# RWKV-7 chunks on TensorE: inversion level 5 and the join over four quarters, decay sum and exponentials moved, 128x128 block products as 64x64 pairs

## The chip, the cores and the metric

The kernel runs on one core of one Trainium2 chip. TensorE (PE) multiplies, VectorE (DVE), ScalarE (ACT) and GpSimd (POOL) do the elementwise work, SyncE (SP) issues most transfers. The metric is the time of one execution in microseconds of the device; lower is better.

## The reference

One layer step of a hybrid decoder: a SwiGLU half step, RWKV-7 time mixing beside an S5 branch, a gated merge, a second SwiGLU half step. 1024 prompt tokens and 8 sample tokens, all in fp32. The change concerns the RWKV branch. Per head of 64 (8 heads):

```python
def step(S, inp):
    r_t, w_t, k_t, v_t, kk_t, b_t = inp
    sa = jnp.einsum('bhvk,bhk->bhv', S, -kk_t)
    S = (S * w_t[:, :, None, :] + sa[..., None] * b_t[:, :, None, :]
         + v_t[..., None] * k_t[:, :, None, :])
    o = jnp.einsum('bhvk,bhk->bhv', S, r_t)
    return S, o
...
mu = jnp.mean(o, axis=-1, keepdims=True)
var = jnp.mean(jnp.square(o - mu), axis=-1, keepdims=True)
o = ((o - mu) * lax.rsqrt(var + LNX_EPS)).reshape(B, L, W) * p['lnx_w'] + p['lnx_b']
bonus = jnp.sum(r_h * k_h * p['r_k'], axis=-1, keepdims=True) * v_h
```

## The kernel before

The prompt is cut into 8 chunks of 128 tokens. Inside a chunk the recurrence is turned into products: masked score matrices of decayed keys (`scores`), the inverse of a unit triangular 128x128 matrix per head, and products with the state. The inverse is built from 2x2 blocks upward. `first` gives blocks of 2; `level_x` and `level_t` do levels 1 to 5, each doubling the block: `level_x` multiplies the score matrix by the inverse so far, DVE copies the masked result into `g.X` (`level`, L2635), `level_t` multiplies again, for the inverse and its transpose, and ACT copies both to `g.T2` (L2373). At level 5 the two 64x64 diagonal blocks are complete; the transposes go to `g.TTF`. `join` (L2919) makes the off-diagonal 64x64 block with two products in a row, each with an ACT copy behind it (`x60`, `x61`, then `t60`, `t61`). Heads are handled as 2 groups n of 4 pairs p; group n owns PSUM banks `tb(n)` and `tb(n)+1` (6, 7 and 4, 5).

The array is used in 64x64 quarters here: a product that reads partitions 0 to 63 or 64 to 127 (`lo`, `hi`) uses that half of the rows, and one that writes PSUM partitions `lo` or `hi` that half of the columns. In `level_x` products go lo to hi and hi to lo. In `level_t` of levels 1 to 4 the first pair crosses and the second stays, so all four quarters are used; in level 5 three products of a pair all cross, two of them hi to lo. The first join product goes lo to hi only, the second hi to lo only. The bonus (`blkrk`), the centring (`T_CEN`) and the sample state sums (`T_BLK`) multiply by 128x128 matrices that are zero outside their two diagonal 64x64 blocks.

The order is written out by hand in a `turn` of each engine, for i from -1 to 8. In turn i the state and outputs of chunk s = i, the inversion of chunk q = i+1 and the preparation of chunk p = i+2 (decays, keys, bonus, gate) are interleaved. Within a turn each engine runs its list in order; semaphores with named events tie the lists. Waits that matter:

- `lora(p)` (L2797) is the first group of a turn on PE. It waits for `bv` of p-1, the bonus values that DVE writes at the end of the turn before (`bonus`, L2615), since both use the same bank.
- On DVE the end of a turn is `level(q,5)`, `decayed_pair(p)`, `inverse_decayed(p)` (event `kr`, which the next `scores` wait for), `bonus(p)`.
- `scores(q,p)` on PE wait for the join's last copy of the chunk before (`t61`), and p = 2, 3 for DVE's mask of p-2. `first(q)` waits for the fourth mask (`score3`).
- DVE's `decay_sum(p)` (L2554) is a running sum over the tokens; it stands between `advance(s)` and `level(q,2)`. ACT's `exps(p)` (L2353) needs it and stands between `level(q,2)` and `level(q,3)`; `decayed_pair(p)` needs the exponentials.
- `new(s)` on PE waits for DVE's `scaled(y)`, the sums (`sums`, L3004) for `rk`, DVE's scaled keys.

## Time and profile before

| | |
|---|---|
| runs | 2399.4, 2398.39, 2395.95 us (median 2398.39) |
| profiled execution | 2397.87 us, its span 2396.1 us |
| PE | busy 2353.7 us (98% of the span) |
| DVE, ACT, POOL | busy 1366.3, 715.0, 1230.1 us |
| granted clock of PE | 0.994 on the mean |
| RWKV stage | turns -1 to 8 from 1233.6 to about 1543 us of the span; turns 0 to 5 last 34.8 to 35.3 us each |

A busy engine is not an engine at its peak: records of matmuls overlap, so the distance between the starts of two groups tells more than the length of a record. A fp32 matmul shows as two records. A line of the timeline merges neighbours of one kind.

### The profile page before, as it was taken

The page shows a single profiled execution, that of the slowest core. Times are in us where ns is not written, and L with a number is a line of the kernel's source. Part 1 is how long each engine was busy: PE and PEld are TensorE (multiplying, and loading weights), DVE is VectorE, ACT ScalarE, POOL GpSimd, SP SyncE. Part 2 cuts the span into 40 slices and gives each one's busy share as a digit, 9 for nine tenths or more (in the row PEclk, how much of TensorE's full clock was granted, in tenths as well). Part 3 has the DMA queues.
Part 4 walks back from the last instruction along what each step waited for, and adds up shares of the span by engine and source line. Part 5 has one row for each costly group of instructions (what it writes and reads, how often), then busy time and mean ns, then how long its engine had stood idle before and what let it go on. Part 6 is the DMA issues. An engine that isn't in the chain of part 4 may idle for free. (4 is left out here: it accounts for less than half of the span.)

```text
span 2396.1 us, 51987 instructions
## 1 busy us (share of the span) xinstructions
PE 2353.7 (98%) x21980; PEld 2299.4 (96%) x21980; DVE 1366.3 (57%) x1939; ACT 715.0 (30%) x1358; POOL 1230.1 (51%) x846
## 2 busy tenths in 40 slices
PE   8999999999999999999999999999999999999998
PEld 8999999999999999999988888899999999999997
DVE  6666666588754455652566665576744444552235
ACT  6433333311020000112446766223433333330001
POOL 3868787644443345223322212254778777765640
PEclk9999999999999999999999999999999999999999
DMA  5212222433333523833451010262222222153212
GB/s 212 92 62 82 85 88 88 177 126 126 106 119 138 107 89 125 152 91 122 152 178 34 19 34 4 96 235 80 80 80 79 79 79 79 61 199 102 78 47 71
DMA packets 121703, 242.83 MB, mean 101 GB/s; under 512 B 35640, under 2 KB 61880, under 8 KB 120896
## 3 DMA queue, kind: packets, MB, share of 16 engines
q1 hardware_dynamic: 94128, 189.67, 24.1%
q10 hardware_dynamic: 27408, 50.76, 6.9%
q8 instruction: 126, 2.06, 0.4%
q14 instruction: 41, 0.34, 0.0%
HBM read 173.94 MB, written 65.29 MB: 100 GB/s over the span
## 5 line engine op out<-in xcount | busy, mean ns | idle before, releaser
L172 POOL TENSOR_TENSOR whi<-wraw,small 128x1024 fp32r<-128x1024 f32 (+1 forms) x60 | 105.2, 1753 | 407.7 <-PE ps L206 316.2
L206 PE MATMUL ps<-hhi,whi 128*128 128x344 f32 x816 | 177.2, 326 | 0.0
L206 PE MATMUL ps<-hlo,whi 128*128 128x344 f32 x816 | 173.6, 321 | 0.0
L206 PE MATMUL ps<-hhi,wlo 128*128 128x344 f32 x816 | 173.0, 320 | 0.0
L4053 PE MATMUL ps<-t_hi,whi 128*128 128x258 f32 x704 | 143.7, 285 | 3.0 <-ACT ffn_gate L3960 1.0
L175 POOL TENSOR_TENSOR wlo<-wraw,whi 128x1024 fp32r<-128x1024 f32 (+1 forms) x60 | 144.1, 2402 | 4.7
L4053 PE MATMUL ps<-t_lo,whi 128*128 128x258 f32 x704 | 142.1, 283 | 0.0
L4053 PE MATMUL ps<-t_hi,wlo 128*128 128x258 f32 x704 | 141.3, 282 | 0.0
L933 PE MATMUL ps<-t_hi,whi 128*128 128x258 f32 x672 | 136.4, 284 | 2.7 <-ACT ffn_gate L829 1.3
L206 PEld LDWEIGHTS ps<-hhi,whi 128*128 128x128 f32 x816 | 136.4, 189 | 2.1 <-issue 0.7
L206 PEld LDWEIGHTS ps<-hlo,whi 128*128 128x128 f32 x816 | 138.4, 190 | 0.0
L206 PEld LDWEIGHTS ps<-hhi,wlo 128*128 128x128 f32 x816 | 137.0, 189 | 0.0
L933 PE MATMUL ps<-t_lo,whi 128*128 128x258 f32 x672 | 135.6, 283 | 0.0
L933 PE MATMUL ps<-t_hi,wlo 128*128 128x258 f32 x672 | 134.9, 282 | 0.0
L933 PE MATMUL ps<-b_hi,whi 128*128 128x258 f32 x576 | 117.6, 286 | 9.4 <-DVE b_lo L561 8.5
L3736 POOL TENSOR_TENSOR wlo<-weights_sum,whi 128x512 fp32r<-128x512 f32 x66 | 92.2, 1397 | 52.6 <-ACT whi L3932 51.4
L933 PE MATMUL ps<-b_lo,whi 128*128 128x258 f32 x576 | 116.8, 284 | 0.0
L933 PE MATMUL ps<-b_hi,wlo 128*128 128x258 f32 x576 | 116.1, 283 | 0.0
L4053 PEld LDWEIGHTS ps<-t_hi,whi 128*128 128x128 f32 x704 | 108.7, 189 | 5.0 <-POOL wlo L3736 1.7
L1007 PE MATMUL ps<-a_hi,whi 128*128 128x344 f32 x528 | 111.8, 320 | 0.0
L1007 PE MATMUL ps<-a_lo,whi 128*128 128x344 f32 x528 | 111.5, 319 | 0.0
L1007 PE MATMUL ps<-a_hi,wlo 128*128 128x344 f32 x528 | 111.3, 319 | 0.0
(607 smaller groups left out, 6692.2 us busy)
## 6 DMA issues: line engine op xcount, KB each, us to landing
weights_raw_b<-ffn_up SPq DMA_DIRECT2D x22, 1024.0 KB, 5.0
wraw<-ffn_up SPq DMA_DIRECT2D x21, 1024.0 KB, 4.9
a_spilled<-ffn_gate SPq DMA_DIRECT2D x39, 516.0 KB, 2.7
a_raw<-a_spilled SPq DMA_DIRECT2D x39, 516.0 KB, 4.1
wraw<-ffn_down SPq DMA_DIRECT2D x48, 384.0 KB, 3.2
wraw<-w_mix SPq DMA_DIRECT2D x18, 512.0 KB, 3.5
gates<-gate_out ACTq DMA_DIRECT2D x16, 516.0 KB, 3.5
wraw<-w_gates SPq DMA_DIRECT2D x16, 512.0 KB, 3.9
```

The lines of the kernel that those rows point to most:

```text
L172: pool.tensor_tensor(g.whi[:, s, 0:n], g.wraw[:, s, 0:n], g.zero.to_broadcast([P, n]), ALU.add).then_inc(g.w_hi, 1)
L175: pool.tensor_tensor(g.wlo[:, s, 0:n], g.wraw[:, s, 0:n], g.whi[:, s, 0:n].bitcast(F32), ALU.subtract).then_inc(g.w_split, 1)
L206: last = pe.matmul(g.ps[:, 3 * bank_set + b, 0:BLK], w[:, s, k * P:(k + 1) * P], x(k, b), start=(k == 0 and first), stop=(k == kt - 1 and ...
L933: last = pe.matmul(g.ps[:, b0 + c, 0:QB], w(k), x[:, k, c * QB:(c + 1) * QB], start=start and k == 0 and fresh, stop=k == DT // 2 - 1 and ...
L1007: last = pe.matmul(g.ps[:, b0 + c, 0:BLK], w[:, s, n * P:(n + 1) * P], x[:, c * BLK:(c + 1) * BLK], start=n == tiles[0] and fresh, stop=n ...
L3736: pool.tensor_tensor(ring(g.wlo, n), source(n), ring(g.whi, n).bitcast(F32), ALU.subtract).then_inc(g.st_lo, 1)
L4053: last = pe.matmul(g.ps[:, b0 + c, 0:QB], ring(w, r, k), x[:, k, c * QB:(c + 1) * QB], start=start and k == 0 and first, stop=k == DT // 2 ...
```

## The change

It does these things:

- Level 5: `level_x` keeps pairs 2 and 3 in their own half (`stays`), so its products use four quarters. `level_end` takes the place of `level_t(5)`: 14 matmuls for a group of heads in place of 12, on all quarters, the fullest of which gets 5 matmuls, before 8. So that this fits, the products of levels 1 to 4 are written to other columns (`levels`), the copies `T2` hold the transposes turned by two pairs (`turned`), and the transposed products of pairs 2 and 3 of level 4 cross halves in place of staying.
- The join: the first product alternates between two quarters and goes to bank 2, for both groups, with one event `x6` and one ACT copy; ACT's copies to `g.TTF` come ahead of that copy. The second product and its copy (`joined`) move to the next turn: on PE behind `lora`, ahead of `scores`; on ACT ahead of the decays. It alternates between two quarters too.
- DVE's `decay_sum(p)` moves between the second and the third mask of the scores; ACT's `exps(p)` between the first and the second token copy.
- Bonus, centring, sample state sums and sample centring: each 128x128 product becomes two 64x64 products, rows and columns lo, rows and columns hi, into the same bank.

```diff
--- before.py
+++ after.py
@@ -2023,9 +2023,10 @@
 
 LEAD = {"act": ["sq", "th", "x"]}
 PRE = {"pe": ["lora", "gate", "bc", "bonus"],
-       "act": ["tw", "la", "ta", "gate", "exp"],
+       "act": ["tw", "la", "ta", "exp", "gate"],
        "dve": ["mid", "rk", "kr", "bv"]}
-JOIN = ["x60", "x61", "t60", "t61"]
+JOIN = ["x6", "t6"]
+SWAP = (0, 2, 1, 3)
 INV = {"pe": SCORES + ["m0", "m1", "tok0"] + XT[0:2] + ["tok1"] + XT[2:6] + ["tok2"] + XT[6:] + JOIN,
        "act": ["tok0", "tok1", "t10", "t11", "tok2"] + [f"t{j}{n}" for j in range(2, 6) for n in range(2)] + JOIN,
        "dve": SCORES + ["m0", "m1"] + [f"x{j}{n}" for j in LEVELS for n in range(2)]}
...
@@ -2183,6 +2184,24 @@
 
     def tb(n):
         return 6 - 2 * n
+
+    def turned(p):
+        return (p + 2) % 4
+
+    def levels(n, j):
+        at = (tb(n) * 8 + (2 if j == 4 else 4)) * N
+        return g.ps[:, :, :].rearrange("p b c -> p (b c)")[:, at:at + 8 * N]
+
+    def ends(n, first, size):
+        return g.ps[:, tb(n):tb(n) + 2, first * N:(first + size) * N]
+
+    def inverse(n, p):
+        at = (3 * (p // 2) + p % 2) * N
+        return g.T2[lo, n].rearrange("p x a c -> p (x a c)")[:, at:at + N]
+
+    def low_end(n, p):
+        at = (5 if p < 2 else 2) * N
+        return g.T2[lo, n].rearrange("p x a c -> p (x a c)")[:, at:at + N]
 
     def prep_bank(d):
         return 0 if d else 6
@@ -2378,22 +2397,27 @@
             for n in range(2):
                 inv["pe"].wait(act, c, f"t{j}{n}")
                 if j < 5:
-                    ins = act.activation(g.T2[:, n].rearrange("p x a c -> p x (a c)"),
-                                         g.ps[:, tb(n):tb(n) + 2, 0:4 * N], ACT.Copy)
+                    ins = act.activation(g.T2[:, n].rearrange("p x a c -> p (x a c)"), levels(n, j), ACT.Copy)
                 else:
-                    act.activation(flat(g.T2[lo, n, 0]), g.ps[lo, tb(n), 0:4 * N], ACT.Copy)
-                    for r in (lo, hi):
-                        ins = act.activation(g.TTF[r, c % 2, 4 * n:4 * n + 4, r], half(tb(n) + 1, 0)[r], ACT.Copy)
+                    ins = act.activation(g.T2[lo, n].rearrange("p x a c -> p (x a c)")[:, 0:6 * N]
+                                         .rearrange("p (b c) -> p b c", b=2), ends(n, 0, 3)[lo], ACT.Copy)
                 q_ev.on(ins, f"t{j}{n}")
 
         def join(c):
 
             for n in range(2):
-                inv["pe"].wait(act, c, f"x6{n}")
-                q_ev.on(act.activation(flat(g.XJ[hi, n]), g.ps[hi, tb(n), 0:4 * N], ACT.Copy), f"x6{n}")
-            for n in range(2):
-                inv["pe"].wait(act, c, f"t6{n}")
-                q_ev.on(act.activation(g.TTF[lo, c % 2, 4 * n:4 * n + 4, hi], half(tb(n), 1)[lo], ACT.Copy), f"t6{n}")
+                for r in (hi, lo):
+                    act.activation(g.TTF[r, c % 2, 4 * n:4 * n + 4, r].rearrange("p (b a) c -> p b a c", b=2),
+                                   ends(n, 3, 2)[r].rearrange("p b (a c) -> p b a c", a=2), ACT.Copy)
+            inv["pe"].wait(act, c, "x6")
+            q_ev.on(act.activation(g.XJ[:, :, :, :].rearrange("p n a c -> p (n a c)"), g.ps[:, 2, 0:4 * N], ACT.Copy),
+                    "x6")
+
+        def joined(c):
+
+            inv["pe"].wait(act, c, "t6")
+            q_ev.on(act.activation(g.TTF[lo, c % 2, :, hi].rearrange("p (m b) c -> p b m c", b=2),
+                                   g.ps[lo, 6:8, 0:4 * N].rearrange("p b (m c) -> p b m c", m=4), ACT.Copy), "t6")
 
         def norm_in(k):
             norm["pe"].wait(act, k, "sums")
@@ -2439,6 +2463,8 @@
             sam["act"].on(act.activation(flat(g.so[:, :, :]), g.ps[:, 6, 0:4 * NB], ACT.Copy), "sq")
 
         def turn(i, s, q, p, d, y):
+            if s is not None:
+                joined(s)
             if p is not None:
                 decay(p)
                 rate_in(p)
@@ -2449,12 +2475,15 @@
             if q is not None or s is not None:
                 bonus_bias(i + 1)
             if p == NCH:
+                exps(p)
                 gate(p)
-                exps(p)
             if s is not None:
                 sa(s)
             if q is not None:
                 tok(q, 0)
+            if p is not None and p < NCH:
+                exps(p)
+            if q is not None:
                 tok(q, 1)
                 level(q, 1)
             if p is not None and p < NCH:
@@ -2470,8 +2499,6 @@
             if q is not None:
                 tok(q, 2)
                 level(q, 2)
-            if p is not None and p < NCH:
-                exps(p)
             if q is not None:
                 level(q, 3)
             if s == NCH - 1:
...
@@ -2635,7 +2662,12 @@
         def level(c, j):
             for n in range(2):
                 inv["pe"].wait(v, c, f"x{j}{n}")
-                st.do(v.copy_predicated(g.X[:, j - 1, n], mask(j), half(tb(n), 0)))
+                if j < 5:
+                    st.do(v.copy_predicated(g.X[:, j - 1, n], mask(j), half(tb(n), 0)))
+                else:
+                    st.do(v.copy_predicated(g.X[:, j - 1, n].rearrange("p (b a) c -> p b a c", b=2),
+                                            mask(j).rearrange("p (b a) c -> p b a c", b=2),
+                                            ends(n, 0, 2).rearrange("p b (a c) -> p b a c", a=2)))
                 q_ev.mark(v, f"x{j}{n}")
 
         def advance(i):
@@ -2699,7 +2731,7 @@
             if q is not None:
                 for n in range(4):
                     scores(q, n)
-                    if last and n == 0:
+                    if p is not None and n == (0 if last else 1):
                         decay_sum(p)
             if last:
                 key(p)
@@ -2728,8 +2760,6 @@
                                     ALU.subtract).then_inc(g.ya_split, 1)
             if last:
                 bonus(p)
-            if p is not None and not last:
-                decay_sum(p)
             if q is not None:
                 level(q, 2)
             if p is not None and not last:
@@ -2843,8 +2873,9 @@
                 pre["dve"].wait(pe, d, "rk")
             w = width(d)
             for p in part:
-                last = pe.matmul(g.ps[:, prep_bank(d), p * CH:p * CH + w], g.blkrk[:, p, :], RK[:, p, 0:w],
-                                 start=True, stop=True)
+                for q in range(2):
+                    last = pe.matmul(g.ps[rows(q), prep_bank(d), p * CH:p * CH + w], g.blkrk[rows(q), p, rows(q)],
+                                     RK[rows(q), p, 0:w], start=True, stop=True)
             if part[-1] == 3:
                 p_ev.on(last, "bonus")
 
@@ -2864,7 +2895,7 @@
             KR = g.KR[:, c % 2]
             if p < 2:
                 pre["dve"].wait(pe, c, "kr")
-                inv["act"].wait(pe, c - 1, "t61")
+                inv["act"].wait(pe, c - 1, "t6" if p else "x6")
             else:
                 inv["dve"].wait(pe, c, f"score{p - 2}")
             for x, src in enumerate((g.K, g.B)):
@@ -2896,39 +2927,82 @@
                     inv["dve"].wait(pe, c, f"m{n}")
                 else:
                     inv["act"].wait(pe, c, f"t{j - 1}{n}")
-                for p in range(4):
+                for p in SWAP:
                     for r, other in ((lo, hi), (hi, lo)):
-                        last = pe.matmul(g.ps[other, tb(n), p * N:(p + 1) * N], g.SC[r, c % 2, 4 * n + p, 1, 0, r],
-                                         T[r, n, 0, p, :], start=True, stop=True)
+                        stays = j == 5 and p >= 2
+                        at = (p - 2 if stays else p) * N
+                        last = pe.matmul(g.ps[r if stays else other, tb(n) + stays, at:at + N],
+                                         g.SC[r, c % 2, 4 * n + p, 1, 0, r], T[r, n, 0, p, :], start=True, stop=True)
                 q_ev.on(last, f"x{j}{n}")
 
         def level_t(c, j):
             T = g.T0 if j == 1 else g.T2
             for n in range(2):
                 inv["dve"].wait(pe, c, f"x{j}{n}")
-                for p in range(4):
+                to = levels(n, j)
+                for p in SWAP:
+                    k = p if j == 1 else turned(p)
                     for r, other in ((lo, hi), (hi, lo)):
-                        if j < 5 or r == lo:
-                            pe.matmul(g.ps[r, tb(n), p * N:(p + 1) * N], T[other, n, 1, p, :],
-                                      g.X[other, j - 1, n, p, :], start=True, stop=True)
+                        pe.matmul(to[r, p * N:(p + 1) * N], T[other, n, 1, k, :], g.X[other, j - 1, n, p, :],
+                                  start=True, stop=True)
+                    at = (4 + turned(p)) * N
                     for r, other in ((lo, hi), (hi, lo)):
-                        last = pe.matmul(g.ps[other if j < 5 else r, tb(n) + 1, p * N:(p + 1) * N],
-                                         g.X[other, j - 1, n, p, :], T[other, n, 1, p, :], start=True, stop=True)
+                        last = pe.matmul(to[r if j == 4 and p >= 2 else other, at:at + N], g.X[other, j - 1, n, p, :],
+                                         T[other, n, 1, k, :], start=True, stop=True)
                 q_ev.on(last, f"t{j}{n}")
 
+        def level_end(c):
+
+            for n in range(2):
+                inv["dve"].wait(pe, c, f"x5{n}")
+
+                def pair_of(p, r):
+                    home = (r if p >= 2 else (hi if r == lo else lo))
+                    return g.X[home, 4, n, p, :], g.T2[home, n, 1, turned(p), :]
+
+                def to(r, b, k):
+                    return g.ps[r, tb(n) + b, k * N:(k + 1) * N]
+
+                for p in SWAP:
+                    X, T = pair_of(p, lo)
+                    pe.matmul(to(lo, p // 2, p % 2), T, X, start=True, stop=True)
+                for p in SWAP:
+                    X, T = pair_of(p, hi)
+                    pe.matmul(to(hi, p // 2, 3 + p % 2), X, T, start=True, stop=True)
+                for p in SWAP:
+                    X, T = pair_of(p, lo)
+                    last = pe.matmul(to(lo, p // 2, 3 + p % 2), X, T, start=True, stop=True)
+                for p in (1, 3):
+                    X, T = pair_of(p, hi)
+                    last = pe.matmul(to(lo, 1 - p // 2, 2), X, T, start=True, stop=True)
+                q_ev.on(last, f"t5{n}")
+
         def join(c):
+            if c:
+                state["dve"].wait(pe, c - 1, "s")
+            if c == NCH - 1:
+                sam["dve"].wait(pe, 0, "u3")
             for n in range(2):
                 inv["act"].wait(pe, c, f"t5{n}")
-                for p in range(4):
-                    last = pe.matmul(g.ps[hi, tb(n), p * N:(p + 1) * N], g.SC[lo, c % 2, 4 * n + p, 1, 0, hi],
-                                     g.T2[lo, n, 0, p, :], start=True, stop=True)
-                q_ev.on(last, f"x6{n}")
+                for p in PAIRS:
+                    at = (2 * n + p // 2) * N
+                    last = pe.matmul(g.ps[lo if p % 2 else hi, 2, at:at + N], g.SC[lo, c % 2, 4 * n + p, 1, 0, hi],
+                                     inverse(n, p), start=True, stop=True)
+            q_ev.on(last, "x6")
+
+        def joined(c):
+
+            inv["act"].wait(pe, c, "x6")
             for n in range(2):
-                inv["act"].wait(pe, c, f"x6{n}")
-                for p in range(4):
-                    last = pe.matmul(g.ps[lo, tb(n), (4 + p) * N:(5 + p) * N], g.XJ[hi, n, p, :],
-                                     g.TTF[hi, c % 2, 4 * n + p, hi], start=True, stop=True)
-                q_ev.on(last, f"t6{n}")
+                for p in PAIRS:
+                    at = (2 * n + p // 2) * N
+                    if p % 2:
+                        last = pe.matmul(g.ps[lo, 7, at:at + N], g.XJ[lo, n, p // 2, :], low_end(n, p),
+                                         start=True, stop=True)
+                    else:
+                        last = pe.matmul(g.ps[lo, 6, at:at + N], g.XJ[hi, n, p // 2, :],
+                                         g.TTF[hi, c % 2, 4 * n + p, hi], start=True, stop=True)
+            q_ev.on(last, "t6")
 
         def head(x, p, q):
             return x[:, (2 * p + q) * N:(2 * p + q + 1) * N]
@@ -2997,7 +3071,9 @@
         def centre(i, half):
             out["act"].wait(pe, i, "o")
             cols = slice(2 * CH * half, 2 * CH * half + 2 * CH)
-            last = pe.matmul(g.ps[:, 1, cols], g.rtab[:, T_CEN, :], flat(g.osq[:, :, :])[:, cols], start=True, stop=True)
+            for q in range(2):
+                last = pe.matmul(g.ps[rows(q), 1, cols], g.rtab[rows(q), T_CEN, rows(q)],
+                                 flat(g.osq[:, :, :])[rows(q), cols], start=True, stop=True)
             if half:
                 o_ev.on(last, "centre")
 
@@ -3045,11 +3121,13 @@
             else:
                 state["dve"].wait(pe, NCH - 2, "s")
             sam["pool"].wait(pe, 0, f"t{p}")
-            sam["pe"].on(pe.matmul(g.ps[:, 2, :], g.rtab[:, T_BLK, :], flat(g.sT[:, p * NB:(p + 1) * NB, :]),
-                                   start=True, stop=True), f"sa{p}")
+            for q in range(2):
+                last = pe.matmul(g.ps[rows(q), 2, :], g.rtab[rows(q), T_BLK, rows(q)],
+                                 flat(g.sT[rows(q), p * NB:(p + 1) * NB, :]), start=True, stop=True)
+            sam["pe"].on(last, f"sa{p}")
 
         def sample_o():
-            inv["act"].wait(pe, NCH - 1, "t61")
+            inv["act"].wait(pe, NCH - 1, "t6")
             sam["dve"].wait(pe, 0, "s3")
             for p in range(4):
                 for b in range(NB):
...
@@ -3082,6 +3162,8 @@
                 merged_early(1, (1,))
             if p is not None:
                 lora(p)
+            if s is not None:
+                joined(s)
             if i == -1:
                 pe.wait_ge(g.set_free[1], up_used)
             if q is not None:
@@ -3160,7 +3242,7 @@
             if p is not None and not last:
                 bonus(p, (0, 1))
             if q is not None:
-                level_t(q, 5)
+                level_end(q)
             if p is not None and not last:
                 bonus(p, (2, 3))
             if q is not None:
```

## Rows read from the trace of the kernel before

**Rows 1.** Table by stretches: busy us of each engine, clock, DMA; steady turn.
```profile
1334.00:1369.00 35.00, 34.56 (x834) 29.94 (x832) 22.00 (x39) 24.74 (x65) 6.79 (x15) 1.00 0.12 30
```

**Rows 2.** Timeline of PE, turn's end: start us, us, line, tiles, forms, records.
```profile
1361.76 0.43 PE L3014 MATMUL ps<-rw_e,rw_tab 128*32 128x128 f32 x8
...
1362.34 1.15 PE L2901 MATMUL ps<-rw_t,rw_scores 64*64 64x64 f32 x32
...
1364.06 0.27 PE L2912 MATMUL ps<-rw_x,rw_t 64*64 64x64 f32 x1
...
1366.06 0.71 PE L2846 MATMUL ps<-rw_e,rw_blkrk 128*128 128x128 f32 x4
...
1367.95 1.27 PE L2929 MATMUL ps<-rw_tt,rw_xj 64*64 64x64 f32 x15
1369.15 1.16 PE L2808 MATMUL ps<-rw_lora,rw_wa 64*128 64x128 f32 x16
```

**Rows 3.** Timeline of PE: the same turn's first group.
```profile
1334.07 1.16 PE L2808 MATMUL ps<-rw_lora,rw_wa 64*128 64x128 f32 x16
```

**Rows 4.** Timeline of DVE, end of the turn, with idle time before.
```profile
1363.07 1.04 DVE L2638 COPY_PREDICATED rw_x<-rw_tab,ps 128x256 f32<-128x256 int32 x2 [0.62 <-PE ps L2901]
...
1367.61 0.69 DVE L2552 TENSOR_TENSOR rw_bv<-ps,rw_f 128x512 f32<-128x512 f32 x1 [0.16 <-DVE rw_b L2612]
```

**Rows 5.** Timeline of PE, levels 2 to 4 of the same turn.
```profile
1353.99 0.27 PE L2912 MATMUL ps<-rw_x,rw_t 64*64 64x64 f32 x2
...
1356.79 0.70 PE L3000 MATMUL ps<-rw_osq,rw_tab 128*128 128x256 f32 x2
1357.42 0.27 PE L2912 MATMUL ps<-rw_x,rw_t 64*64 64x64 f32 x2
...
1358.51 0.49 PE L2832 MATMUL ps<-rw_norm,rw_sel 64*128 64x128 f32 x4
...
1360.46 0.27 PE L2912 MATMUL ps<-rw_x,rw_t 64*64 64x64 f32 x2
```

**Rows 6.** Timeline of PE, end of turn 6.
```profile
1505.38 1.13 PE L3048 MATMUL ps<-sm_tmp,rw_tab 128*128 128x512 f32 x2
1506.44 1.15 PE L2901 MATMUL ps<-rw_t,rw_scores 64*64 64x64 f32 x32
...
1513.67 0.44 PE L2947 MATMUL ps<-rw_s_apart,rw_kr 128*64 128x128 f32 x4
```

**Rows 7.** Timeline of PE, start of turn -1.
```profile
1233.59 1.16 PE L2808 MATMUL ps<-rw_lora,rw_wa 64*128 64x128 f32 x16 [1.81 <-issue]
...
1241.20 0.34 PE L2883 MATMUL ps<-rw_b,rw_kr 64*64 64x64 f32 x8 [0.53 <-DVEq L2013]
```

**Rows 8.** Timeline of DVE, turn -1: third and fourth mask.
```profile
1238.49 2.60 DVE L2552 TENSOR_TENSOR rw_scores<-ps,rw_tab 128x1024 f32<-128x1024 f32 x2 [0.15 <-DVE rw_scores L2552]
```

**Rows 9.** Timeline of ACT, end of the steady turn: copies of the inverse.
```profile
1365.53 0.76 ACT L2386 ACTIVATE rw_tt<-ps 64x256 f32<-64x256 f32 x2
```

**Rows 10.** Timeline of DVE, steady turn: masks and decay sum.
```profile
1340.02 2.60 DVE L2552 TENSOR_TENSOR rw_scores<-ps,rw_tab 128x1024 f32<-128x1024 f32 x2 [1.28 <-PE ps L2872]
...
1350.59 1.37 DVE L2561 TENSOR_TENSOR_SCAN rw_cum<-seg,rw_e 128x128 f32<-128x128 f32 x4
...
1352.08 0.16 DVE L2566 TENSOR_SCALAR rw_small<-rw_cum 128x4 f32<-128x4 f32 x1
```

**Rows 11.** Timeline of PE, steady turn: the first inversion product.
```profile
1342.94 0.34 PE L2883 MATMUL ps<-rw_b,rw_kr 64*64 64x64 f32 x8
```

**Rows 12.** Timeline of ACT, steady turn: second token copy, exponentials.
```profile
1348.57 0.60 ACT L2371 ACTIVATE rw_tok<-ps 128x512 f32<-128x512 f32 x1 [3.25 <-PE ps L2859]
...
1355.86 1.28 ACT L2361 ACTIVATE rw_fall<-rw_cum,rw_small 128x129 f32<-128x129 f32 x4
...
1358.22 0.19 ACT L2364 ACTIVATE rw_small<-rw_small 128x4 f32<-128x4 f32 x1
```

**Rows 13.** Table by stretches: the sample outputs and what follows.
```profile
1525.40:1535.60 10.20, 9.29 (x66) 8.72 (x65) 5.39 (x16) 1.89 (x7) 0.00 (x0) 0.50 0.19 56
```

10 lines of the change are left out of this document (6 added, 4 removed).

## Prediction

> **What bounds the kernel now.** I first read the busy shares of the page and the table by stretches. TensorE (PE) is busy for 34.56 of 35 us in a steady turn of the RWKV stage, at the full clock, while VectorE (DVE) has 22.0 and ScalarE (ACT) 24.7 [rows 1]. The rest of the kernel is untouched, and every engine waits at the end of the stage, so I take what this stage gains or loses as what the kernel gains or loses. Then I read one turn on PE's timeline, from its first LoRA product at 1334.07 to the next at 1369.15: 35.08 us [rows 2, 3]. PE hardly idles in it, so I cost every edit as PE time first. The reader is then to see the second thing in the same stretch on DVE: after the last level copies (L2638, 1363.07) DVE does 5.23 us of work without a pause and ends with the bonus values at 1368.30 [rows 4], and the next LoRA product (L2800) waits for exactly that. Today PE comes 0.85 us after it. That slack decides this change.
>
> **Prices of PE, from rows.** A fp32 matmul shows as two records. A level's first product (32 records, 16 in each of two quarters of the array) takes from 1362.34 to 1363.42, 1.08 us; level 5's second product (48 records, of which 32 go to the one quarter from rows hi to columns lo) takes from 1364.06 to 1366.06, 2.00 us [rows 2]; an ordinary second product has 64 records, 16 in each of four quarters, and takes from 1357.42 to 1358.51, 1.09 us [rows 5]. These fit one rule: the fullest quarter counts, 0.058 us for each record of 64 columns, and about 0.16 us come on top where the tile shape changes between neighbours. A record of 256 columns: the 512-column product takes 1.06 us for two records [rows 6], the 256-column centring product 0.63 us for two [rows 5]; the difference of 0.43 us is two times 256 columns, so 0.215 us each and again 0.20 us for the change of shape.
>
> **The change, part by part.** I call X the start of level 5's first product (1362.34).
>
> *Level 5 and join.* Level 5's first product uses four quarters: 8 records deep instead of 16, 0.47 us less. Its second product has 28 matmuls in the two halves, 10 on the fullest quarter: 20 records deep instead of 32, 0.70 us less. The join's first part goes from 16 records in one quarter to 8 deep; its second part (L2929, today 1.20 us [rows 2]) leaves this place. The bonus products as 64x64 pairs cost the same per column but no change of shape, about 0.3 us less for each of two. By PE alone, lora would start at X + 3.4 instead of X + 6.81. It can't: it waits for DVE. DVE's level copies start 4 records (0.23 us) earlier, because the first half of the product is half as deep; then the same 5.23 us follow [rows 4]. So the bonus values are ready at X + 5.73. From DVE's end to PE's next product I find 0.11 us (1241.09 to 1241.20 [rows 7, 8]) when the shape stays; I take 0.11 to 0.20 and set lora at X + 5.92, and add 0.05 for the copies' new address pattern. **Gain 0.87 us a turn**, not 3.4; PE idles about 2.4 us there.
>
> *The moved half of the join* now sits between lora and the scores. 16 records on two quarters: 8 x 0.058 = 0.47 us, plus 0.16, plus a second change of shape for the scores behind it, 0.19: **+0.81 us a turn**. ScalarE's copy that it needs follows four 0.38 us copies [rows 9], and is ready at about X + 4.8, before lora ends; so nothing is added there. The copy of its result (0.6 us) now stands ahead of the decay's activations, which all scores and the decay sum can bear (the sum needs them 3.7 us after the scores start, they end after 2.4).
>
> *Decay sum between the score masks.* Today the sum runs from 1350.59 to 1352.24 [rows 10], where DVE then waits for PE anyway. It needs 1.80 us with its two gaps. Between the second and third mask DVE has 1.28 us free [rows 10], of which 0.15 is the ordinary gap [rows 8]: 1.12 us hide, 0.68 do not. PE's first inversion product waits for the fourth mask, which ends at 1342.62; it starts at 1342.94 [rows 11], so 0.12 to 0.21 us more hide: **+0.50 us a turn**, between 0 (if I misjudge what PE waits for) and 0.7. Queued behind DVE's sum are the two masks and, behind them, all of the inversion. In the turn before the first state (i = -1) there is no pause: the masks run back to back and PE waits for them [rows 7, 8], so all 1.80 us show, once.
>
> *Exponentials.* They leave the place between the copies of levels 2 and 3 (1355.86 to 1358.41) and go into ScalarE's wait of 3.25 us ahead of the second token copy [rows 12]: 2.55 us, hidden. If they had stayed, the faster centring below would have waited for the level-3 copy. In turn -1 that wait is 1.8 us, so about 0.5 us show, once.
>
> *Centring as 64x64 pairs.* The stretch from level 2's second product to the key scale runs from 1353.99 to 1358.51, 4.52 us, with five groups of two shapes [rows 5]. As one shape: 3 x 0.93 + 2 x 0.43 + 0.16 = 3.83 us. ScalarE's copies of level 2 end 0.05 us before PE wants them, so it holds: **-0.69 us a turn**, in the six turns that have both.
>
> *Level 4.* For pairs 2 and 3 both products go through the two crossing quarters: 24 records deep instead of 16, +0.47 us. Today this group takes 1.30 us (1360.46 to 1361.76) against 1.09 at level 3 [rows 2, 5], because the sums behind it wait 0.21 us for DVE's scaled keys. That wait is covered: **+0.25 us a turn**.
>
> *Last turns.* In turn 6 there is no bonus chain on DVE. The merged bonus group (small columns) loses 0.5 us, the four 512-column sample products lose their changes of shape, level 4 costs 0.4, and from 1505.38 to r0 at 1513.67 (8.29 us [rows 6]) I count 7.15 with the join's first half, the copies (four of 0.38 and one) and its second half, now in line. Together -2.2 us besides the +0.81; turn 7 -0.3.
>
> **The sum.** Seven turn ends: 7 x (-0.87) = -6.1. Moved half: 7 x 0.81 = +5.7. Decay sum: 6 x 0.50 = +3.0, and turn -1 +2.3. Centring: 6 x (-0.69) = -4.1. Level 4: 7 x 0.25 = +1.8. Last turns -2.5. Total +0.1 us. The profiled execution took 2397.87 us (span 2396.1), 0.5 below the median of 2398.39; I forecast **2398.0**. Bounds: -0.6 or +0.2 for the decay sum, +/-0.2 for each of the others in seven turns, and +/-1.5 for the last ones: 2394 to 2402. A change of 0.2% is 4.8 us, about what a measurement can tell.
>
> **A rule against the change.** Level 1 to 4's first products send the two row halves into one PSUM bank, to different partitions, and yet run at 0.058 us per record of a quarter: 32 records in 1.08 us [rows 2]; one after the other they would take 1.9. The new pairs for centring, bonus and sample sums write in just that manner, so the sum lets them overlap. The Trainium skill (TensorEngine Tiling (Array Packing), Gotcha 1: PSUM Pressure) says the opposite: different row tiles cannot access one PSUM bank at the same time. By that rule the pairs would take turns.
>
> **Rivals.** (a) *The pairs take turns at their bank.* Each centring product is then 4 x 0.215 us deep instead of 2, +0.43, twelve times in the steady turns: +5.2; four sample products +3.5, half of it covered; the bonus lies in DVE's shadow. 2398.0 + 7 to 9: 2405 to 2407, slower. It is decided where the pair of row halves writes one bank; the level products speak against it. That is what the skill's rule would give. Chance 0.08.
> (b) *TensorE's clock falls.* PE idles some 2.4 us a turn after a thin join. In the present trace the clock went to 1.2 GHz (granted 0.50) for 10.2 us, 1525.4 to 1535.6 [rows 13], behind the sample outputs, a product whose records stream one column each, though PE was 9.29 us busy in that stretch. A fall of that length costs at least 5 us where PE sets the pace. Against it: an idle time of 1.81 us before turn -1 left the clock at full [rows 7]. One fall: 2403; one a turn: over 2430. Chance 0.08.
> (c) *The decay sum is free.* If DVE's masks are not what PE waits for, 6 x 0.50 + 1.80 + 0.5 us go: 2392.7. Chance 0.14.
> (d) *DVE does not hold lora.* If the chain behind the level copies shrinks or the wait is met early, lora starts at X + 3.4 and the moved half behind it waits some 0.45 us for its copy, so the scores start 2.4 us earlier than today and not 0.06: 7 x 2.3 = 16 us, 2382. The code's wait and the gap of 0.85 us speak against it. Chance 0.08.
>
> **Chances.** My forecast 0.62, (a) 0.08, (b) 0.08, (c) 0.14, (d) 0.08. Faster by over 0.2% (below 2393.6) are (c), (d) and 0.03 of my own case: 0.25. Slower are (a), (b): 0.16. Within: 0.59. The range 2390 to 2404 takes in my case, (c) and a single fall of the clock, and leaves out (a), (d) and the worse part of (b).
>
> **What would show it.** After the change: PE idle of about 2.4 us just before the LoRA product in turns 0 to 6, ended by DVE's bonus values; turn length 35.1 +/- 0.3 us; level 5's second product in about 1.3 us; the stretch from level 2 to the key scale in 3.8 us; level 4's second product in about 1.55 us without idle; 0.5 us of idle before the first inversion product, ended by the masks, and 1.8 us more in turn -1; ScalarE's exponentials followed by a wait before the second token copy. The prediction is wrong if the idle before lora is under 1 us, if the centring pairs take 0.87 us each, or if the granted clock is 0.5 in a steady turn.

## The result, and the profile after

| | before | changed |
|---|---|---|
| median, beside each other | 2396.7 us (2395.88 to 2399.4) | 2411.04 us (2407.7 to 2412.13) |
| span of the profiled execution | 2396.1 us | 2409.3 us |
| PE busy, granted clock | 2353.7 us, 0.994 | 2344.3 us, 0.989 |

The changed kernel takes 1.0055 of the time before (95% interval 1.0043 to 1.0066): slower by 13 us (the two medians lie 14.3 us apart). That is above the range of 2390 to 2404, and, as the rest shows, it is rival (b), the fall of TensorE's clock.

The table by stretches of the changed kernel, one line for each turn from -1 to 5 (columns as in [rows 1]):

```profile
1233.90:1265.60 31.70, 24.06 (x652) 20.30 (x653) 18.86 (x33) 20.72 (x55) 4.27 (x7) 1.00 0.28 82
1265.60:1302.30 36.70, 33.36 (x844) 28.50 (x844) 20.14 (x36) 24.82 (x63) 7.15 (x16) 0.95 0.11 28
1302.30:1337.50 35.20, 32.06 (x852) 27.78 (x853) 22.14 (x39) 24.81 (x63) 6.80 (x15) 1.00 0.12 29
1337.50:1374.40 36.90, 33.73 (x852) 29.08 (x853) 22.14 (x39) 24.83 (x63) 6.77 (x15) 0.95 0.11 29
1374.40:1411.90 37.50, 33.81 (x853) 29.07 (x853) 22.13 (x39) 24.81 (x63) 6.80 (x15) 0.95 0.11 28
1411.90:1448.30 36.40, 33.63 (x854) 28.92 (x854) 22.15 (x39) 24.82 (x63) 6.80 (x15) 0.94 0.11 29
1448.30:1485.80 37.50, 34.86 (x854) 30.10 (x854) 22.00 (x39) 24.12 (x63) 7.08 (x15) 0.91 0.04 4
```

The clock column is the reading. Turn 1 (1302.3 to 1337.5) has the full clock and lasts 35.2 us, as before (35.08) and as forecast (35.1 +/- 0.3). The other turns from 0 to 5 have 0.91 to 0.95 and last 36.4 to 37.5; turn -1 (31.7 us, 30.63 before) keeps the full clock too. A stretch inside such a turn shows what the mean hides; the second line is the same place in the undisturbed turn:

```profile
1338.40:1341.80 3.40, 3.40 (x32) 2.71 (x30) 0.00 (x0) 1.80 (x6) 2.28 (x6) 0.50 0.02 5
1303.40:1306.80 3.40, 3.40 (x54) 2.79 (x54) 1.42 (x2) 2.61 (x8) 2.12 (x6) 1.00 0.03 7
```

The numbers behind x count the matmul records of the stretch: at 1.2 GHz (0.50) PE gets through 32 in 3.4 us, where it gets through 54 at 2.4 GHz. From turn -1 to turn 6 the clock is low six times: from 1266.7, 1338.4, 1375.9 and 1413.5 for 3.4 us each, from 1447.6 and 1485.1 for 6.8 us, 27.2 us together. Before the change it was never low there. What PE did before a fall stands in its waits between 1234 and 1540 us (line waited for: us in total, times, longest):

```profile
PE ps L2838 <- issue: 16.6, 7, 2.5
...
PE ps L2838 <- DVEq L2013: 2.2, 1, 2.2
```

L2838 is the lora product. PE idles in front of it in turns 0 to 6 for 2.23 to 2.54 us each (the first line also counts the 1.6 us before turn -1; "issue" means that the profile names no releaser), and every fall begins between 0.7 us before and 1.6 us after such a lora product; only the one at 1302.34 has no fall behind it. Behind the wait of 1.6 us before turn -1 (1.81 before, [rows 7]) the clock stayed at full here.

DVE at the same turn end, the lines that answer to [rows 4]:

```profile
1332.01 1.03 DVE L2668 COPY_PREDICATED rw_x<-rw_tab,ps 128x256 f32<-128x256 int32 x2 [0.65 <-PE ps L2934]
1333.26 0.82 DVE L2579 TENSOR_TENSOR rw_kr<-rw_e,rw_fall 128x512 f32<-128x512 f32 x1 [0.22 <-DVE rw_x L2668]
...
1334.81 0.77 DVE L2579 TENSOR_TENSOR rw_k<-rw_e,rw_e 128x512 f32<-128x512 f32 x1
...
1336.68 0.69 DVE L2579 TENSOR_TENSOR rw_bv<-ps,rw_f 128x512 f32<-128x512 f32 x1 [0.16 <-DVE rw_b L2639]
```

And PE's groups of turn 1 that answer to [rows 2, 5 and 11], at full clock but for the last line, which already holds the beginning of a fall:

```profile
1312.48 0.34 PE L2914 MATMUL ps<-rw_b,rw_kr 64*64 64x64 f32 x8 [0.38 <-DVEq L2013]
...
1323.53 0.27 PE L2946 MATMUL ps<-rw_x,rw_t 64*64 64x64 f32 x2
...
1324.52 0.60 PE L3075 MATMUL ps<-rw_osq,rw_tab 64*64 64x256 f32 x4
1324.94 1.00 PE L2934 MATMUL ps<-rw_t,rw_scores 64*64 64x64 f32 x26
...
1327.44 0.49 PE L2862 MATMUL ps<-rw_norm,rw_sel 64*128 64x128 f32 x4
...
1329.36 0.27 PE L2946 MATMUL ps<-rw_x,rw_t 64*64 64x64 f32 x2
...
1330.90 0.43 PE L3090 MATMUL ps<-rw_e,rw_tab 128*32 128x128 f32 x8
...
1331.48 0.69 PE L2934 MATMUL ps<-rw_t,rw_scores 64*64 64x64 f32 x32
1332.01 0.60 PE L2877 MATMUL ps<-rw_e,rw_blkrk 64*64 64x128 f32 x8
...
1337.53 1.35 PE L2838 MATMUL ps<-rw_lora,rw_wa 64*128 64x128 f32 x16 [2.50 <-issue]
```

Each term of a turn can be read off as a distance between starts. X is 1331.48:

| term | forecast | measured in turn 1 |
|---|---|---|
| X to lora | -0.87 (to X + 5.92 or 5.97) | -0.76 (X + 6.05, before X + 6.81) |
| moved half of the join (lora to the first state product) | +0.81 | +0.81 (3.63 against 2.82) |
| decay sum (state product to first inversion product) | +0.50 | +0.45 (1.54 against 1.08) |
| level 2 to the key scale | -0.69 | -0.61 (3.91 against 4.52) |
| level 4's second product | +0.25 | +0.24 (1.54 against 1.30) |

The five add up to +0.13, and the turn is 0.10 longer. So the sum held in the one turn with a full clock, and the loss should be the clock's. The experiments try that.

### The profile page after: what moved, and what is told of

Same layout as the page of the kernel before. It is cut to its first block and busy times, and to the rows that moved or that the text cites. A ratio compares the mean times of both kernels' runs of the same rounds, so it can differ in the third digit from the quotient of the medians.

```text
span 2409.3 us, 52334 instructions
## 1 busy us (share of the span) xinstructions
PE 2344.3 (97%) x22158; PEld 2290.8 (95%) x22158; DVE 1368.3 (57%) x1939; ACT 716.1 (30%) x1342; POOL 1229.1 (51%) x846
## 5 line engine op out<-in xcount | busy, mean ns | idle before, releaser
L541 POOL TENSOR_TENSOR whi<-wraw,small 128x768 fp32r<-128x768 f32 (+1 forms) x30 | 43.9, 1462 | 133.9 <-PE ps L1007 124.6
```

Source lines behind the costliest of these rows:

```text
L541: pool.tensor_tensor(g.whi[:, s, 0:n], g.wraw[:, s, 0:n], g.zero.to_broadcast([P, n]), ALU.add)\
```

## The experiments

My theory: PE's idle stretch before lora lets the clock fall, and without it the changed kernel would take what the sum gave. The rival: something else in the change (the 64x64 quarters, the pairs, the new order) costs the time or lowers the clock. Each run is compared with runs of the kernel before on the same chip, whose medians were 2397.45 to 2398.38 us; the ratio is not exactly that of the two medians (fill2: 1.0001, the medians give 1.0007).

| kernel | median us | ratio (95%) |
|---|---|---|
| fill | 2397.94 | 1.0002 (0.9992 to 1.0011) |
| fill2 | 2399.84 | 1.0001 (0.9992 to 1.0011) |
| idle | 2430.57 | 1.0138 (1.0122 to 1.0155) |
| level5 | 2405.93 | 1.0033 (1.0021 to 1.0046) |
| pairs | 2397.48 | 0.9994 (0.9985 to 1.0004) |
| nopairs | 2411.42 | 1.0063 (1.0047 to 1.0080) |
| nodecay | 2409.83 | 1.0051 (1.0034 to 1.0068) |
| fill_nopairs | 2403.58 | 1.0023 (1.0014 to 1.0033) |
| fill_nodecay | 2397.97 | 1.0000 (0.9991 to 1.0010) |
| early | 2389.7 | 0.9967 (0.9957 to 0.9977) |
| early2 | 2386.2 | 0.9951 (0.9934 to 0.9968) |
| earlyb | 2399.62 | 1.0004 (0.9994 to 1.0013) |

**fill: the changed kernel with PE kept at work.** Five products that nobody reads, in front of lora.

```diff
@@ turn of PE, behind join(q)
+                if not last:
+                    for _ in range(5):
+                        pe.matmul(g.ps[:, 3, 0:2 * CH], g.rtab[:, T_CEN, :],
+                                  g.rtab[:, 0:2, :].rearrange("p a c -> p (a c)"), start=True, stop=True)
```

> The kernel after, with five more 128x128 products of 256 columns on PE behind the join, into bank 3, whose contents nobody reads again: PE work of 5 x 0.43 = 2.15 us in the place where it idles 2.2 to 2.5 us in front of the LoRA products of turns 0 to 6. Nothing else is changed, and the output is the same. Theory 'idle' (the idle time in front of lora lets TensorE's clock fall): the granted clock stays full in turns 0 to 5, the turns last 35.2 us each as the one without a fall does, and the kernel takes 2396 to 2400 us. Theory 'thin' (the products of level 5, the join and the pairs, now spread over four quarters, lower the clock by themselves): falls in the steady turns remain, 2407 us or more. Theory 'prices' (my per-turn terms were wrong and the clock is a side matter): the time stays at 2405 to 2411 with a full clock.

It took 2397.94 us, 13 less than the changed kernel, with more work. PE's timeline in front of lora, and the table by stretches over three turns:

```profile
1333.10 2.43 PE L3252 MATMUL ps<-rw_tab 128*128 128x256 f32 x10
1335.70 1.16 PE L2838 MATMUL ps<-rw_lora,rw_wa 64*128 64x128 f32 x16 [0.17 <-issue]
```

```profile
1300.00:1335.00 35.00, 34.23 (x863) 29.44 (x862) 21.94 (x40) 24.72 (x63) 6.60 (x15) 1.00 0.12 30
1335.00:1370.00 35.00, 34.20 (x863) 29.42 (x862) 21.95 (x39) 24.72 (x63) 6.67 (x14) 1.00 0.12 30
1370.00:1405.00 35.00, 34.20 (x863) 29.41 (x862) 22.08 (x39) 24.73 (x63) 6.58 (x15) 1.00 0.12 29
```

The 2.5 us of idle time are now 2.43 us of filler and 0.17 of idle, the clock stays at 1.00, and turns 1 to 4 last 35.17 to 35.18 us. From the lora of turn -1 to the first product of the merge the changed kernel takes 328.06 us, this one 315.40, the kernel before 315.21. The difference is 12.66 us; half of the 27.2 us of low clock is 13.6. Not all of it is the falls' own. Some 1.5 us lie in the last wait, where DVE needs a transfer for the merge (the changed kernel, then fill):

```profile
1560.62 1.23 DVE L3394 SCALAR_TENSOR_TENSOR merge_t<-merge_in,ps 128x1032 f32<-128x1032 f32 x1 [3.78 <-DMA merge_in<-wb]
1546.76 1.23 DVE L3398 SCALAR_TENSOR_TENSOR merge_t<-merge_in,ps 128x1032 f32<-128x1032 f32 x1 [2.31 <-DMA merge_in<-wb]
```

Early and early2 have the longer wait too (3.92 us in early), with fewer falls, so it isn't shown to come from them. That leaves 11.2 us for 27.2 us of low clock, about 0.4 of it. The 0.2 us between fill and the kernel before agree with the +0.1 of my sum, but in part by luck (see below).

**fill2: two fillers in place of five.**

```diff
@@ turn of PE, behind join(q)
+                if not last:
+                    for _ in range(2):
+                        pe.matmul(...)
```

> The changed kernel with two filler products instead of five behind the join, so that of the 2.3 us ahead of lora about 1.5 stay idle. If it is the length of that idle stretch that lets the clock fall, there are fewer falls than the changed kernel's seven in turns -1 to 6, or none: 2398 to 2403. If any stretch of over 1 us does it, falls as there: 2409 to 2411. If the filler kernel was faster for another reason than its full TensorE queue, no value of this kernel is excluded.

2399.84 us. PE's waits for lora in this kernel:

```profile
PE ps L2838 <- issue: 9.9, 7, 1.6
...
PE ps L2838 <- DVEq L2013: 1.2, 1, 1.2
```

It still idles 1.1 to 1.5 us in front of each steady lora, and the clock is 1.00 in each turn from -1 to 5, which last 35.05 to 35.35 us from turn 1 on. (The expectation speaks of seven falls of the changed kernel; its trace has six there.) So it isn't any idle time that costs: seven stretches of up to 1.5 us lose nothing in this trace, seven of 2.2 to 2.5 us lose 11 us or more. That is no sharp bound. In early2 below, the clock fell 1.4 us into the lora of turn 0, in front of which PE had idled only 1.32 us; in early, behind the same 1.32 us, it did not.

**idle: the kernel before, with the idle time and nothing else of the change.** Four repeats of DVE's step for K make lora late.

```diff
@@ decayed_pair(d), behind the step for g.K
+            if 0 < d < NCH:
+                for _ in range(4):
+                    tt(g.K[:, :, :], E7[:, :, :], EX[:, :, :], ALU.mult)
```

> The kernel before, with DVE repeating its product K four times (the same values again) at the end of each of seven turns: 4 x 0.84 = 3.36 us ahead of the bonus values. PE's slack of 0.85 us less its wake of 0.15 is used up, so lora comes about 2.6 us later, behind an idle PE; levels, join and pairs are the old ones. Theory 'idle': 7 x 2.6 = 18 us of waiting, and besides the clock falls in most of these turns: 2422 to 2430 us. Theory 'thin': the waiting alone, clock full in turns 0 to 5: 2413 to 2417 us.

2430.57 us. The lora of turn 2 and what DVE did in front of the next:

```profile
1343.87 0.59 PE L2811 MATMUL ps<-rw_lora,rw_wa 64*128 64x128 f32 x2 [2.48 <-issue]
```

```profile
1377.03 4.03 DVE L2552 TENSOR_TENSOR rw_k<-rw_e,rw_e 128x512 f32<-128x512 f32 x5
```

The four repeats are 3.2 us (4 x 0.81), of which 0.85 were slack, so a turn should be 2.4 us longer: 37.5. Turns 0 to 5 last 38.97 to 40.78, 15.0 us more than six times 37.5. A low stretch of 3.4 or 6.8 us stands at each of the seven turn starts from 1265 to 1504 (1265.1, 1302.6, 1343.6, 1381.1, 1422.1, 1463.0, 1504.0), 34.5 us of it within these six turns, so the 15.0 us are a little under half of it. None of the quarters, pairs or new orders is in this kernel. The idle stretch alone makes the clock fall.

**level5: the kernel before with level 5, the join and level 4's new columns alone.** The pairs, the decay sum and the exponentials stay as before.

> The kernel before with only the level 5 and join part (and the level 4 that it needs). By my prices per turn: -0.87 at the turn's end (DVE's chain), +0.81 for the moved half of the join, +0.25 for level 4: +0.2 us a turn, +1.3 in seven, -1 in the last: 2397 (2395 to 2400) with a full clock. PE idles about 1.8 us in front of lora; theory 'idle' sees perhaps some falls (1.7 us each for 3.4 us at half the clock), and 'thin' too.

2405.93 us, a miss by 9: I had written this expectation for a full clock. Turns 3 and 5, without a fall, last 35.35 and 35.23 us against 35.08, which is about the +0.3 of my terms (-0.76 + 0.81 + 0.24). Turn 2 lasts 36.72 at a clock of 1.00 too: PE pauses for 0.93 us inside its output products (L3049), a pause that comes back below. PE waits for lora

```profile
PE ps L2839 <- issue: 12.7, 6, 2.1
PE ps L2839 <- DVEq L2013: 1.7, 1, 1.7
```

and four of the seven loras have a fall of 3.4 us (from 1263.4, 1300.9, 1410.2, 1481.8), the first behind an idle stretch of 1.67 us only. So this part by itself turns a kernel whose PE is full into one that loses its clock, in some turns.

**nopairs and nodecay: the changed kernel with one part undone.** nopairs writes the four products as single 128x128 ones again; nodecay puts `decay_sum` and `exps` back:

```diff
--- after (nopairs, centre; bonus and the sample products alike)
-            for q in range(2):
-                last = pe.matmul(g.ps[rows(q), 1, cols], g.rtab[rows(q), T_CEN, rows(q)],
-                                 flat(g.osq[:, :, :])[rows(q), cols], start=True, stop=True)
+            last = pe.matmul(g.ps[:, 1, cols], g.rtab[:, T_CEN, :], flat(g.osq[:, :, :])[:, cols], start=True, stop=True)
--- after (nodecay, turn of DVE)
-                    if p is not None and n == (0 if last else 1):
+                    if last and n == 0:
                         decay_sum(p)
...
+            if p is not None and not last:
+                decay_sum(p)
             if q is not None:
                 level(q, 2)
```

> The kernel after with the 64x64 pairs undone: bonus, centring, sample sums and sample centring are 128x128 products again. By my prices 0.69 us come back in each of six turns (4.1 us) and about 1.3 us in the last ones; the bonus lies in DVE's shadow and costs nothing, but shortens PE's idle time in front of lora from 2.4 to 1.8 us. With the clock falling as in the kernel after: 2411 + 5 = 2416. If the shorter idle time is short enough to keep the clock (theory 'idle' allows it, 1.8 us in front of turn -1 did no harm): 2403 to 2406. Theory 'thin': fewer falls too, since the wide products are back. If the pairs had cost time (their halves taking turns at the bank): under 2409.

> The kernel after with decay sum and exponentials back where they were. By my prices the decay sum between the masks costs 0.50 us in six turns and 1.8 + 0.5 us in turn -1: 5.3 us. Against it, level 3's copies then wait for the exponentials on ScalarE, since the centring pairs let PE arrive 0.7 us earlier: about 0.4 us come back in each of six turns. Together 2 to 4 us less than the kernel after, if the clock behaves the same: 2407 to 2409. Theory 'idle' sees no change of the idle time in front of lora and expects falls as before.

2411.42 and 2409.83 us: neither removes the loss, and in both, six of the seven steady loras have a fall. In nodecay the idle stretches are 2.23 to 2.53 us; in nopairs they are 1.67 to 2.14, as in level5, and the one of 1.67 has no fall. nopairs has a seventh fall in turn -1 (1241.4), 0.6 us behind a wait of 2.3 us for the masks. Since each draws its own number of falls, their medians say nothing of what the undone part costs. That needed a pair of kernels at full clock.

**fill_nopairs and fill_nodecay: the same two, with fillers** (four and five).

> The filler kernel (full clock) with the 64x64 pairs of the centring undone, four fillers in place of five. This reads the pairs' own price at full clock, which nopairs could not show under its falls. If the forecast's 0.69 us a turn holds and TensorE binds that stretch: 2397.9 + 7 x 0.65 = 2402.5 (2401.5 to 2403.5), gap ahead of lora 0.2 us. If, as the kernel with the pairs alone suggests, a part of it is lost: 2399 to 2401.

> The filler kernel with the decays' sum and their exponentials put back to where they stood before the change. The sum between the masks cost 0.45 us a turn at the masks and some 1.3 us more in turn -1; the exponentials early bring 0.61 us at the key scale. If both are real: 2397.9 - 7 x 0.45 - 1.3 + 7 x 0.6 = 2397.6 (2396 to 2399), turns of 35.3, turn -1 of about 29.9. If the early exponentials bring nothing on the chain: 2393 to 2395. If the sum costs nothing there: 2401 to 2402.

2403.58 us: without the pairs 5.6 us more than fill (5.0 when each is held against the kernel before on its own chip). A turn is 35.79 against 35.18, 0.61 us; turn -1 is 32.28 against 31.58, with a low stretch at 1243.0 in it. The pairs are worth 0.61 us a turn at full clock, and all of it lies from level 2 to the key scale: 4.52 us again, against 3.91.

2397.97 us: without the moved sum and exponentials nothing changes in the end. Turns are 35.37 us instead of 35.18, turn -1 is 30.07 instead of 31.58, and a low stretch of 3.4 us at 1511.9, which fill has not, takes back its half. So the moved sum and exponentials together win 0.19 us in a steady turn and lose 1.5 once. The trace shows both parts: without the moved sum the first inversion product comes 1.08 us after the state product and not 1.53, and with the exponentials in their old place PE waits 0.54 us for level 3's copy, so the faster centring wins nothing.

**pairs: the kernel before with the pairs alone.**

> The kernel before with only the 64x64 pairs. Here PE still sets the pace in front of lora (slack of DVE's bonus values 0.85 us less 0.15 of wake), and the bonus pairs save 0.3 us each: 0.6 us a turn fit into the slack of 0.7. The centring would save 0.69, but level 3's copies wait for the exponentials: 0.3 to 0.4 remain. About 0.9 to 1.0 us in each of six turns, 0.6 in turn -1, 1.5 in the last ones: 2397 - 8 = 2389 (2387 to 2392). PE hardly idles, so theory 'idle' expects the full clock in the steady turns; theory 'thin' allows falls. If the pairs' halves take turns at their bank: 2397 + 5 or more.

2397.48 us, a miss by 8. The steady turns are 34.65 us, 0.43 less where I expected 0.9 to 1.0. PE's lines of turn 2, from 1332.48 to 1367.13, tell which part is missing:

```profile
1357.36 1.16 PE L2902 MATMUL ps<-rw_t,rw_scores 64*64 64x64 f32 x32 [0.54 <-ACT rw_t L2381]
...
1360.75 0.97 PE L2902 MATMUL ps<-rw_t,rw_scores 64*64 64x64 f32 x26
...
1367.13 1.16 PE L2808 MATMUL ps<-rw_lora,rw_wa 64*128 64x128 f32 x16
```

X (1360.75) stands 28.27 us behind lora, just as before the change. With the exponentials still between ACT's copies of levels 2 and 3, PE waits for the level-3 copy, and the whole gain of the centring goes into that wait; I had let 0.3 to 0.4 us of it remain. From X to the next lora it is 6.38 us against 6.81: this 0.43, where I expected 0.6, is all that the pairs bring here.

The profiled execution took 2394.0 us, 3.8 less than the kernel before, but the median of the runs does not show that. The granted clock of each execution, which is on record, tells why in part: the four that took 2392.5 to 2394.0 us had a mean of 0.994 or 0.995, five that took 2397.3 to 2399.1 us had 0.991 to 0.993 (the tenth, 2400.07 us, had 0.964), and the kernel before 0.993 to 0.996. So most executions of pairs lost their gain together with some of the clock. The trace has a low stretch of 6.8 us at 1471.6 that the kernel before has not, with no idle time in front of lora. Where the clock fell in the slower executions, and why, stays open.

**early: what the theory says should be done.** If DVE's chain makes PE idle, shorten the chain: K, the second half of `KR` and the copy of the last decay need only the exponentials, which are there early since the change. They move behind level 3, where DVE has time.

```diff
+        def early(d):
+            pre["act"].wait(v, d, "exp")
+            inv["pe"].wait(v, d - 1, "tok2")
+            if d >= 2:
+                state["pe"].wait(v, d - 2, "o")
+                second(d)
+            tt(g.K[:, :, :], E7[:, :, :], EX[:, :, :], ALU.mult, False)
+            st.do(v.tensor_copy(g.rs[:, R_END[d % 2], 0:4], g.fall[:, :, CH]))
...
-            inv["pe"].wait(v, d - 1, "tok2")
-            tt(g.K[:, :, :], E7[:, :, :], EX[:, :, :], ALU.mult)
-            st.did(v.tensor_copy(g.rs[:, R_END[d % 2], 0:4], g.fall[:, :, CH]))
@@ turn of DVE, behind level(q, 3)
+                else:
+                    early(p)
```

> The kernel after, with three DVE steps moved: the decayed queries (KR second half, 0.78 us), K (0.77 us) and the copy of the chunk's end decay (0.30 us) are made behind level 3's copies, where DVE idles 1.9 us, instead of behind level 5's (in turn -1 the queries stay, since their buffer is in use). Same output. If DVE's chain from level 5's copies to the bonus values is what holds lora, lora comes 1.85 us earlier in turns 0 to 6, PE idles about 0.6 us there instead of 2.4, and by theory 'idle' the clock stays full: 2398 - 7 x 1.85 = 2385 us (2383 to 2388). Theory 'thin': the same 13 us less, but the falls remain: 2395 to 2399. If something else holds lora: no gain, 2409 to 2411.

2389.7 us, 0.33% under the kernel before and 21 us under the changed one, though 5 us short of what I expected. The idle stretch is 0.3 to 0.8 us (1.32 in turn 0), no clock falls in turns 0 to 5, which last 33.3 to 33.8 us, but for one of 34.59 (it has a pause at L3065, the output products, of 0.94 us). One low stretch of 3.4 us stands in turn -1, from 1241.6, at the end of a wait of 2.3 us for the masks.

**early2: the sum taken apart.** Three of its four scans between masks 2 and 3, the fourth and the scalars behind mask 4.

```diff
@@ turn of DVE, early's
-                    if p is not None and n == (0 if last else 1):
-                        decay_sum(p)
+                    if last and n == 0:
+                        decay_sum(p)
+                    if p is not None and not last and n == 1:
+                        decay_sum(p, (0, 1, 2))
+                    if p is not None and not last and n == 3:
+                        decay_sum(p, (3,))
```

> The early kernel with the sum of the decays taken apart: the first three scans stand between score masks 2 and 3, the fourth and the scalars behind mask 4. If the masks that wait behind the four scans are what lengthened the span from the state product to the next stage's first product by 0.45 us (1.54 against 1.08), each turn is 0.3 to 0.45 us shorter than in early (33.3 to 33.8) and turn -1 by about 0.7: 2386.5 (2385 to 2388). If it is the exponentials, which still wait for the fourth scan, that hold the stage, nothing is gained: 2389 to 2391. The gap ahead of lora stays at 0.3 to 0.8 us, and no low clock from turn 0 to turn 4.

2386.2 us. DVE around the masks, PE at the next lora, and one turn of the table by stretches:

```profile
1302.29 2.60 DVE L2579 TENSOR_TENSOR rw_scores<-ps,rw_tab 128x1024 f32<-128x1024 f32 x2
1305.03 0.42 DVE L2588 TENSOR_TENSOR_SCAN rw_cum<-seg,rw_e 128x128 f32<-128x128 f32 x1
```

```profile
1361.98 1.26 PE L2860 MATMUL ps<-rw_lora,rw_wa 64*128 64x128 f32 x16 [0.78 <-issue]
```

```profile
1328.98:1361.98 33.00, 31.97 (x853) 27.76 (x853) 21.94 (x39) 25.22 (x65) 5.68 (x14) 1.00 0.12 32
```

Turns 2, 4 and 5 last 33.0 us, 2.1 less than before the change (turn 1 is 33.5, turn 3, with a pause of 0.98 us in the output products, 34.3, and turn 0, with a low stretch at 1261.8, 35.1). Turn 2 took 33.6 in early, and PE's wait of 0.38 us for the masks is gone: they are what PE waited for. This kernel has the lowest ratio of the study, 0.9951, though on four runs its interval meets that of early.

**earlyb: the control.** The same three steps moved in the kernel before.

> The kernel before with the same three VectorE steps (KR1, K, the copy to R_END) moved behind level 3: the control of early. Before the change TensorE reached lora last and had no gap, so VectorE's early end is worth nothing there: 2397 (2395 to 2399). If the order of VectorE's work is worth something by itself, whatever the change did to TensorE: 2390 to 2393.

2399.62 us, no gain; the turns are 35.28 us, even 0.2 longer (the sums behind level 4's second product wait for DVE), and there is one low stretch of 3.4 us at 1478.0, with no idle time in front of lora. Without the change PE reaches lora last, and DVE's early end is worth nothing. So the change does make room, and only DVE's chain kept it from being used.

## Why the prediction was wrong

**What bounds the stage: right.** PE now reaches lora before DVE's bonus values, and the idle stretch of about 2.4 us that I named is there (2.23 to 2.54).

**The sum of a turn: right; the sum of the stage: right in part by luck.** Fill, the changed kernel with its clock kept up, took 2397.94 us where I forecast 2398.0, and all five terms of a turn are within 0.11 us (the key-scale term adds up to 3.81 us, not to the 3.83 that I wrote; it measured 3.91). Three places outside of them were off and cancelled. In turn -1 the moved sum and exponentials cost 1.5 us and not 2.3 (30.07 against 31.58). From turn 6's lora to the merge fill gained 2.4 us (71.85 against 74.22), where my terms give 0.81 - 2.5 = -1.7. Against these two, turn 0 was 36.21 us in fill, 1.0 more than the others, with a pause of PE that my sum has not:

```profile
1283.53 0.32 PE L3049 MATMUL ps<-rw_kr,rw_s_apart 128*64 128x128 f32 x1 [1.06 <-issue]
```

A pause of 0.3 to 1.1 us stands in the output products of one or two turns (0, 2 or 3) in every trace with the new level 5 but that of fill_nopairs; in the changed kernel it is turn 3, 0.88 us. None of the four kernels with the old level 5 (before, idle, pairs, earlyb) has one. So it seems to have come with the change, at up to 1 us; its cause is open.

**Rival (a): refuted.** The first centring pair (L3075 above) runs from 1324.52 to the next start at 1324.94. These 0.42 us are two records of 256 columns (0.43), not four (0.86), and fill_nopairs shows the pairs to be worth 0.61 us a turn. Both row halves write one bank at once. The Trainium skill (TensorEngine Tiling (Array Packing), Gotcha 1: PSUM Pressure) rules that out; for fp32 products to different partitions the measurement decides against it.

**Rival (b): it is what happened, and it names the step that failed.** The sum booked the new idle time of 2.4 us in front of lora at nothing beyond the wait itself, with TensorE at full clock throughout; the clock fell behind six of seven such stretches, for 27.2 us together. I gave that a chance of 0.08 on one row, the idle time of 1.81 us before turn -1 that left the clock at full [rows 7]. That row is one stretch, shorter than the 2.4 us that I had just computed, and it stands once. The new idle time is longer and returns every 35 us. I took a row from beside the case for a bound of the case. Its price was mis-sized too, in the other direction: I took the fall of 10.2 us behind the sample outputs [rows 13], so "one a turn: over 2430", where the falls here last 3.4 or 6.8 us and cost about half of that or a little less: turns 2 to 4, with one of 3.4 us each, are 1.7, 1.4 and 1.2 us longer than turn 1 (turn 3 without its pause of 0.88 us). At half of 27.2 us the rival would have stood at 2398 + 13.6 = 2411.6, against 2411.04 measured, and not at over 2430.

**Rivals (c), (d):** the decay sum wasn't free (0.45 us of 0.50 measured, and early2's gain once it was split), and DVE did hold lora. But early2 shows where (d) was worth looking at: the same change with the chain shortened is 12 us faster than the kernel before.

## What to carry to other kernels

If a change makes the bounding engine so fast in one place that it waits for another, don't book the idle time as harmless: here an idle stretch of over 2 us at TensorE in each turn of a loop brought 3.4 or 6.8 us at half the clock behind it in most turns, and cost up to half of those. Look for what ends the wait, and move work out of that chain in the same change: the three steps that early moves turned a loss of 0.55% into a gain of 0.33%. If the chain can't be cut, cheap useless products in the gap can keep the clock, as a filler that leaves 1.1 to 1.5 us did here; and comparisons between variants whose clocks fall differently say nothing of their parts until each is filled.

## What the runs showed of the hardware

- Low clock by idle time in front of lora, seven steady turns each: 1.1 to 1.5 us (fill2) none; 0.3 to 1.32 us (early, early2) none and one, behind 1.32 us; 1.67 to 2.14 us (level5, nopairs) four and six; 2.23 to 2.54 us (the changed kernel, nodecay) six each; 2.47 to 2.52 us (idle) seven. So the length of the stretch alone does not decide it.
- Behind the 1.6 to 1.8 us before turn -1 no trace shows a fall within 9 us. In three of the six kernels in which PE waits 2.3 us for the masks in turn -1 (early, nopairs, fill_nopairs) the clock fell between 0.3 us before and 1.5 us after the end of that wait.
- pairs and earlyb each have one fall behind turn 6's lora with no idle time in front of it (1471.6, 1478.0): idle time there is a cause of falls, not the only one.
- A fall lasted 3.4 or 6.8 us in these turns, though the engine was busy from its start on: 3.40 of 3.40 us in the line of 1338.40.
- A product of 64x64 pairs that writes both partition halves of one bank ran at the speed of one quarter (0.42 us for 256 columns, four records): level 2 to the key scale took 3.91 us against 4.52 with single 128x128 products.
